# Weight pieces of 512 rows by 512 columns in place of 1024 rows by 256 columns, in a one-core streaming encoder step

## What is computed

```python
def trunk_layer(x, k_cache, v_cache, s0, pos0, ...):
    h = rms_norm(x, attn_norm_g)
    proj = h @ w_in                                   # 1024 x 2816
    ...
    x = x + mixed @ w_out                             # 1024 x 1024
    x = x + peer(rms_norm(x, ffn_norm_g), peer_w_q, peer_sub_keys, peer_u, peer_v)

def peer(x, w_q, sub_keys, u_table, v_table):         # for each block of 128 tokens
    q = (xblk @ w_q).reshape(PEER_BLOCK, PEER_HEADS, 2, PEER_HALF)      # 1024 x 2048
    ...                                               # top 16 of 128 keys twice, then top 16 of 256: 128 experts a token
    u = u_table[expert]
    hid = jax.nn.gelu(jnp.einsum('thkd,td->thk', u, xblk).astype(jnp.float32), approximate=False)
    v = v_table[expert]
    return jnp.einsum('thk,thkd->td', (g * hid).astype(xblk.dtype), v)
```

## Time and profile before

| | us |
|---|---|
| median of 3 runs | 3637.41 (3636.71 to 3653.42) |
| the profiled execution, its own time | 3651.41 |
| its span, first to last instruction | 3649.3 |
| busy: PE / PE weight loads / DVE / ACT / POOL | 1989.2 / 1092.7 / 2038.2 / 324.0 / 2103.3 |
| mean rate of the DMA engines over the span | 352 GB/s |
| bytes of the POOL queue (q0) / of SP's queue (q1) | 1140.99 MB / 134.48 MB |

### The profile page before, as it was taken

How to read it: one execution, slowest core, us unless ns; L and a number is a source line. 1 busy time by engine, 2 the same in 40 slices (tenths; PEclk the granted TensorE clock), 3 DMA queues, 4 the chain that set the end, 5 groups by cost and what they waited for, 6 DMA issues and landing times. The chain is left out here.

```text
span 3649.3 us, 27702 instructions
## 1 busy us (share of the span) xinstructions
PE 1989.2 (55%) x9448; PEld 1092.7 (30%) x9448; DVE 2038.2 (56%) x4571; ACT 324.0 (9%) x778; POOL 2103.3 (58%) x2183
## 2 busy tenths in 40 slices
PE   6975563766673447657734367557634332223446
PEld 6764441544550115324501034324301000000001
DVE  2379747567648674674565744755675644444120
ACT  2211010111100010111100010101000000000000
POOL 0045523656556675665566765666676766666665
PEclk9986786886885668768956579668756655655669
DMA  6588965999999999999999999999998999999998
GB/s 224 179 302 287 392 234 184 343 397 355 381 383 376 371 368 395 401 368 367 397 394 353 344 378 394 392 370 394 404 349 328 368 376 375 373 364 386 366 362 323
DMA packets 442170, 1286.15 MB, mean 352 GB/s; under 512 B 39408, under 2 KB 157936, under 8 KB 442032
## 3 DMA queue, kind: packets, MB, share of 16 engines
q0 software_dynamic: 313344, 1140.99, 82.0%
q1 hardware_dynamic: 126224, 134.48, 11.0%
q10 hardware_dynamic: 2464, 8.91, 0.6%
HBM read 1274.50 MB, written 9.44 MB: 352 GB/s over the span
## 5 line engine op out<-in xcount | busy, mean ns | idle before, releaser
L926 DVE CUSTOM_DVE_ANT_0 ring<-ring,ps 128x1024 f32<-128x1024 f32 x1088 | 1298.2, 1218 | 929.7 <-DMA ring<-in_peer_u_dram,u_idx 777.6
L658 POOL DMA_INDIRECT ring<-in_peer_u_dram,u_idx x1088 | 1038.6, 955 | 809.4 <-issue 286.4
L1243 PE MATMUL ps<-ring,spread 128*32 128x512 f32 x4352 | 884.2, 916 | 1122.5 <-DMA ring<-in_peer_v_dram,v_idx 1011.2
L658 POOL DMA_INDIRECT ring<-in_peer_v_dram,v_idx x1088 | 1062.9, 977 | 718.6 <-issue 292.9
L1284 PE MATMUL ps<-wbuf,actT 128*128 128x256 f32 (+1 forms) x2944 | 712.0, 401 | 135.4 <-issue 94.9
L1243 PEld LDWEIGHTS ps<-ring,spread 128*32 128x32 f32 x4352 | 180.5, 143 | 1717.8 <-issue 1700.9
L1284 PEld LDWEIGHTS ps<-wbuf,actT 128*128 128x128 f32 (+1 forms) x2944 | 563.0, 195 | 317.5 <-issue 213.6
L999 DVE MAX8 work<-work 128x8 f32<-128x128 f32 (+3 forms) x432 | 109.6, 325 | 84.5 <-ACT work L895 68.0
L1003 DVE FIND_INDEX8 work<-work 128x8 uint32<-128x128 f32 (+3 forms) x432 | 134.3, 335 | 15.6 <-issue 15.6
L728 ACT COPY spread<-weightT 128x16 f32<-128x16 f32 x64 | 14.0, 219 | 924.6 <-PE ps L1243 487.6
L926 DVE DVE_READ_ACCUMULATOR2_ANT hidden<- 128x1 f32 x1088 | 90.2, 83 | 1.1 <-issue 1.1
(11 more groups left out here) (153 smaller groups left out, 1283.8 us busy)
## 6 DMA issues: line engine op xcount, KB each, us to landing
wbuf<-in_w_in_dram SPq DMA_DIRECT2D x55, 1024.0 KB
wbuf<-in_peer_w_q_dram SPq DMA_DIRECT2D x40, 1024.0 KB
wbuf<-in_w_out_dram SPq DMA_DIRECT2D x20, 1024.0 KB
ring<-in_peer_u_dram,u_idx POOLq DMA_INDIRECT x1088
ring<-in_peer_v_dram,v_idx POOLq DMA_INDIRECT x1088
x_v<-x_scratch ACTq DMA_DIRECT2D x8, 512.0 KB
out_dram<-x_v ACTq DMA_DIRECT2D x8, 512.0 KB
x_in<-in_x_prompt_dram SPq DMA_DIRECT2D x7, 512.0 KB
```

Of the source, the lines that this page charges most:

```text
L658: pool.indirect_dma_start(ring[:, at % RING, :], None, table, bass.IndirectOffsetOnAxis(ap=idx, axis=0)).then_inc(landed[at % RING], 16)
L926: ch.put(v_.tensor_tensor_reduce(out=row, in0=row, in1=ux_ps, scale=1.0, scalar=0.0, op0=ALU.mult, op1=ALU.add, accum_out=hidden[:, k:k + ...
L1243: mm = pe.matmul(ps[j:j + 32, B_ACC + c, :], spread[:, at:at + 32], tile[:, 512 * c:512 * c + 512], start=(t % 32 == 0), stop=(t % 32 == 3 ...
```

## The change

A piece is now half the rows (512) by twice the columns (512), still 1 MB, but 512 runs of 2 KB. A product of 512 columns is made of two half sums: for both blocks the first half of k from one piece, then for both blocks the second half from the next. `w_in` has 2816 columns, so its last 256 columns stay one piece of 1024 rows. There are 23 pieces in a phase as before (11 of `w_in`, 4, 8), 6 + 2 + 4 products of a block in place of 11 + 4 + 8, and half as many matmuls of twice the width. A product fills a whole PSUM bank. The first half's end is signalled by a new semaphore `half_used`, on which SP refills. The copies and adds are 512 columns wide; they come at the point of `Pace` at which the second half of the block is done. `EARLY` is 4 of the 512-column products, `PIECE` is 7.2.

```diff
-WCOLS = 256
-N_IN, N_OUT, N_Q = IN_W // WCOLS, D // WCOLS, 2 * PH * 128 // WCOLS
-PIECES = N_IN + N_OUT + N_Q
+WCOLS = 512
+N_IN, N_OUT, N_Q = -(-IN_W // WCOLS), D // WCOLS, 2 * PH * 128 // WCOLS
 WRING = 3
-EARLY = 8
-EARLY_LOADS = EARLY + 2
+EARLY = 4
...
+def pieces():
+    out = []
+    for name, count, width in (("w_in", N_IN, IN_W), ("w_out", N_OUT, D), ("w_q", N_Q, 2 * PH * 128)):
+        for p in range(count):
+            whole = width - p * WCOLS < WCOLS
+            out += [(name, p, half) for half in ((None,) if whole else (0, 1))]
+    return out
...
-    NORM, PIECE, ATTN, PEER, BEGUN_PEER = 6, 3.6, 55, 105, 58
+    NORM, PIECE, ATTN, PEER, BEGUN_PEER = 6, 7.2, 55, 105, 58
...
-        wbuf = sb("wbuf", [P, WRING, KC, WCOLS])
+        wbuf = sb("wbuf", [P, WRING, KC // 2 * WCOLS])
...
+                elif n >= WRING:
+                    name, p, half = W_PIECES[n - WRING]
+                    if half == 0:
+                        firsts = sum(h == 0 for _, _, h in W_PIECES[:n - WRING + 1])
+                        grp = next(i for i, phase in enumerate(PHASES) if phase[0] == blocks)
+                        sp.wait_ge(half_used, grp * (N_IN - 1 + N_OUT + N_Q) + firsts)
+                    elif name == "w_in":
+                        sp.wait_ge(in_done, N_IN * b0 + (p + 1) * G)
...
-                        th.step("w_in", m, 0.5)
+                        th.step("w_in", p * G, (G + g + 1) / 2)
...
-                        th.step("w_q", m, 0.5)
+                        th.step("w_q", p * G, (G + g + 1) / 2)
...
-                        th.step("w_out", m, 0.5)
+                        th.step("w_out", p * G, (G + g + 1) / 2)
...
+            def products(grp, name, p, blocks, free, signal):
+
+                G = len(blocks)
+                parts = halves(name, p)
+                for i, (n, half) in enumerate(parts):
+                    last = i == len(parts) - 1
                     for g, b in enumerate(blocks):
+                        m, T = p * G + g, rows(b)
+                        th.step(name, p * G, (i * G + g) / len(parts))
+                        if i == 0:
+                            free(g, b, m)
+                        pe.wait_ge(w_landed[n % WRING],
+                                   16 * (grp * len(range(n % WRING, PIECES, WRING)) + n // WRING + 1))
+                        w = w_place(n)
+                        ks = range(KC) if half is None else range(half * (KC // 2), (half + 1) * (KC // 2))
+                        for k in ks:
+                            if k == ks[len(ks) // 2]:
+                                th.step(name, p * G, (i * G + g + 0.5) / len(parts))
+                            mm = pe.matmul(ps[0:T, 2 + m % 2, 0:w.shape[-1]], act_of[b][:, k, 0:T], w[:, k - ks[0], :],
+                                           start=(k == 0), stop=(k == KC - 1), skip_group_check=True)
+                        if last:
+                            mm.then_inc(signal, 1)
+                        elif g == G - 1:
+                            mm.then_inc(half_used, 1)
```

More of the change, by code:

```diff
@@ L66, with halves @@
 RING = 14
+def pieces():
[5 more added lines that the diff above has]
+    return out
+W_PIECES = pieces()
+PIECES = len(W_PIECES)
+IN_PIECES = sum(name == "w_in" for name, _, _ in W_PIECES)
+OUT_PIECES = sum(name == "w_out" for name, _, _ in W_PIECES)
+EARLY_LOADS = 2 * EARLY + 2
+def halves(name, p):
+    return [(n, half) for n, (m, c, half) in enumerate(W_PIECES) if (m, c) == (name, p)]
 SLOPES = [2.0 ** (-8.0 * (h + 1) / HEADS) for h in range(HEADS)]
@@ L292, in hymba_peer_program @@
     u_table, v_table = peer_u[0], peer_v[0]
-    w_views = [w[0].rearrange("(k p) n -> p k n", p=P) for w in (w_in, w_out, peer_w_q)]
+    w_views = {name: w[0].rearrange("(k p) n -> p k n", p=P)
+               for name, w in (("w_in", w_in), ("w_out", w_out), ("w_q", peer_w_q))}
     def w_piece(n):
[L296 to L302, removed]
+        name, p, half = W_PIECES[n]
+        if half is None:
+            return w_views[name][:, :, p * WCOLS:]
+        return w_views[name][:, half * (KC // 2):(half + 1) * (KC // 2), p * WCOLS:(p + 1) * WCOLS]
     def x_rows(b):
@@ L512, in hymba_peer_program @@
         following = PHASES[1][0]
[L513 removed]
+        early_h = {1: 0, 2: 1}
         order = gather_order()
@@ L547, in stream @@
                     m = n - WRING
[L548 to L553, removed]
+                    if m == IN_PIECES:
                         for g, b in enumerate(blocks):
                             if b >= SAMPLE - 1:
-                                th.step("attn", g, 1.0)
                                 store_window_and_state(b)
-                    if m == N_IN + N_OUT:
+                    if m == IN_PIECES + OUT_PIECES:
                         for g, b in enumerate(blocks):
-                            th.step("norm2", g)
                             T = rows(b)
@@ L1263, in h_transposed, with project @@
                     transposed(i, T, lambda c: h_nat[0:T, (4 * i + c) * P:(4 * i + c + 1) * P], 4, h_tr)
-            def project(blocks, grp, pieces):
+            def project(blocks, grp, chunks):
                 G = len(blocks)
-                for p in pieces:
-                    for g, b in enumerate(blocks):
-                        m = p * G + g
-                        th.step("w_in", m)
-                        pe.wait_ge(hT_ready, 2 * b + 2)
-                        if m >= 2:
-                            pe.wait_ge(proj_ready, N_IN * blocks[0] + m - 1)
-                        product(grp, "w_in", 0, p, m, b, in_done)
@@ L1277, in product, with free @@
-            def product(grp, name, first, p, m, b, signal):
-                n, T = first + p, rows(b)
-                pe.wait_ge(w_landed[n % WRING], 16 * (grp * len(range(n % WRING, PIECES, WRING)) + n // WRING + 1))
-                for k in range(KC):
-                    if k == KC // 2:
-                        th.step(name, m, 0.5)
-                    mm = pe.matmul(ps[0:T, 2 + m % 2, 0:WCOLS], act_of[b][:, k, 0:T], wbuf[:, n % WRING, k, :],
-                                   start=(k == 0), stop=(k == KC - 1))
-                mm.then_inc(signal, 1)
+                def free(g, b, m):
+                    pe.wait_ge(hT_ready, 2 * b + 2)
+                    if m >= 2:
+                        pe.wait_ge(proj_ready, N_IN * blocks[0] + m - 1)
```

80 lines of the change are left out of this document (41 added, 39 removed).

## The result

| | before | after |
|---|---|---|
| median of 4 runs, us | 3638.5 (3636.7 to 3653.4) | 3593.5 (3583.1 to 3604.0) |
| the profiled execution / its span, us | 3651.4 / 3649.3 | 3583.1 / 3581.2 |

What follows compares the result with a forecast made beforehand. Bound by the chain of products, attention and top-16 search until about 650 us, then by the DMA engines. Terms: -15 - 4 - 3 + 1 = -21 us, from 3637 to 3616 us; forecast's own range 3600 to 3634, overall 3594 to 3648.

Steps and rivals of the forecast that it cites:

- `w_q`, -3 us: Phase 1's `w_q`, where PE waits for ACT's copies: one product more done by 453 us, -3 us (+7 to -10).
- `w_out`, -4 us: Phase 1's one 4.34 us wait for a `w_out` piece: pieces land in 7.3 us, not 12.1, -4 us (0 to -4).
- Packets, -15 us: Weights from 660 us on: fewer packets, each with a fixed cost of 7.3 ns, -15 us (0 to -31).
- mixed rate: Sign of being right: where weights and gathers fill the DMA queues, the sum rises from 394 to 400 GB/s or more.
- Width of the matmuls, 0 us: PE: four matmuls of 512 columns take the same 3.45 us as eight of 256, no change; upper end +4 us.
- Copies +1, joints, order 0: Wider last copies at step ends in phases 0 and 1 cost +1 us; shifted order of items costs nothing.
- Run length not what limits: Rival: full DMA engines give about 400 GB/s whatever the packets; only phase 1 and copies count, 3631 us, chance 0.22.
- Fewer joints help: Rival: half as many copies joining products save waiting on something unnamed throughout, 25 us more, 3591 us, chance 0.12.
- Stiffer joints: Rival: PE wants the bank sooner after its copy and loses half products in phases 2 to 4, 3659 us, chance 0.16.
- pace of wide matmuls: Sign of being right: on PE, four wide matmuls take 3.45 us.
- phase 1 ends 5 to 10 us earlier: Sign of being right: the end of phase 1 comes 5 to 10 us earlier.
- all of ACT's waits for an unnamed releaser grew: Sign of being wrong: ACT's waits for which the profile names no releaser grow; no size given.

Runs made afterwards that it cites:

- e3: The change's joints, copies and order with 1 KB packets and 256-column matmuls of the kernel before, noisy chip: ratio 1.002 to the kernel before.
- e2: The change with each wide matmul as two of 256 columns, alternating column halves, each with its own start, noisy chip: ratio 1.0004 to the kernel before.
- e1_runs_2k: The change with each piece moved by two DMAs of row halves, still 2 KB packets, noisy chip: ratio 0.9892 to the kernel before.
- e1_runs_1k: The change with each piece moved by two DMAs of column halves, so 1 KB packets, noisy chip: ratio 0.9944 to the kernel before.
- e13: e1_runs_2k again, as control on a quiet chip: 3364.5 us, ratio 0.9862 to the kernel before.
- e11: e13 with 1 KB packets for the weights of phase 1 alone: 3391.0 us, ratio 0.9941 to the kernel before.
- e12: e13 with 1 KB packets for the weights of phases 2 to 4 alone: 3383.7 us, ratio 0.9923 to the kernel before.
- c2: The kernel before, unaltered, run for its profile on a quiet chip: ratio 0.9996.
- e8: The change with each half product as two 256-column halves one behind the other, sums started once a bank, quiet chip: ratio 0.9861 to the kernel before.
- e6: The change with four empty PE instructions ahead of each wide matmul, quiet chip: ratio 0.9859 to the kernel before.
- e9: e3 unaltered on a quiet chip: ratio 0.9994 to the kernel before.
- e7: The change with a matmul of 4 zero columns behind each wide one, quiet chip: ratio 1.0039 to the kernel before.
- e4: The change with each half product as two 256-column halves one behind the other, each with its own start, quiet chip: ratio 0.9861 to the kernel before.

## Why the prediction was wrong

**`w_q`, -3 us: the step that failed.** The prediction let ACT's late copies hold PE until 453 us as before and gave the change one product more by then. In its own pair of executions `w_q` became 28 us shorter, and its unnamed stops fell from 31.9 to 7.1 us. What took them away stays open. It was not that pieces came sooner. The earlier trace rows show it: from 430 to 450 us the weights' queue moved nothing, so the pieces that had been issued had landed, while PE stood the 16.70 us that ended at 453.13. Ahead of the stop of 15.19 us that began at 416.16, the queue moved 10 packets from 405 to 410 us, so the third piece, issued at 390.50 and wanted next, lay ready as well. By the traces of the noisy chips, one execution of each kernel, it goes with the width of the matmuls: the last unnamed stop ends at 453.1, 453.6 and 456.0 us with narrow ones (before, e3, e2), and at 424.5, 443.6 and 443.4 with wide ones (the change, e1_runs_2k, e1_runs_1k).

On the quiet chips, where no such stop exists, the same term fails for a reason that is shown. The pieces are the limit there. From e13 to e11 only the packets of phase 1 differ, and `w_q` is 57.0 and 77.8 us long. The first three pieces lie ready in the ring; the fourth comes 3.1 us late, the next three follow every 12.4 us in place of 7.1, which makes 19 of the 20.8 us; for the last the gathers have run out. The prediction had this arithmetic, 12.1 us a piece with 1 KB and 7.3 with 2 KB, and applied it only to the wait that the trace named, in `w_out`. The Trainium skill ("DMA: Bandwidth & Descriptors", "Queues, rings and completion order") has the rule in general: an engine goes round the queues that have work, a whole packet from each. The trace agrees, 2961 packets to 2962. The page calls 9 to 17 descriptors in a packet typical; equal counts would come out with any number that both queues share, so the trace neither shows nor refutes that.

**`w_out`, -4 us: right.** e11 has a wait of 2.88 us there and begins `w_q` 3.7 us after e13.

**Packets, -15 us: right in kind, somewhat small.** e12 measures 19.2 us for phases 2 to 4. The 7.3 ns for a packet were 9: by the line through three sizes above, and by e12, 19.2 us x 16 over 33,792 packets saved = 9.1 ns. That a 2 KB packet costs the same as one of 1 KB, the term's condition, is shown by that line. The mixed rate rose as foretold, from 394 to 402 GB/s in c2's and the change's stretches. The skill's rule that was weighed against it (the Trainium skill, "DMA: Bandwidth & Descriptors", "Why small descriptors are slow"; an estimate of 9 us) came out too low.

**Width of the matmuls, 0 us: right on the quiet chips, not on the noisy one.** Four wide ones take 6.87 / 2 = 3.43 us in phase 0 against 3.45 forecast, and e8 equals the change. (The upper end counted 20 wide half products in phase 0; there are 22, which makes no difference to the sum.) On the chip of e1 to e3, e2 loses everything that the packets give: the term put at nothing is there as large as the whole gain. Two limits would fit, late completions of products with narrow matmuls and, once they are gone, late pieces; this is argued, not shown. Why completions are late on some chips, and less so with half the matmuls, no run here shows; e6 was meant to and could not. e2 also alternates column halves and gives their starts in its own way, and neither was taken out on a noisy chip.

**Copies +1, joints, order 0: right.** e9 gives -0.1%, within its interval, and e3 +0.2%. DVE's add behind "weights" and the stiffer joints cost no more than that.

**The rivals.** "Run length not what limits" is refuted by the table of four. "Fewer joints help" had the right time, 3591, by luck, and the wrong cause: the joints alone give nothing. "Stiffer joints" did not happen. Of the signs listed, the packets, the mixed rate, the pace of wide matmuls and the tail came as said; "phase 1 ends 5 to 10 us earlier" did not, it was 40, and that line pointed at the failed step. One sign of being wrong came too: all of ACT's waits for an unnamed releaser grew, from 735.5 to 866.4 us, though those of the product copies fell from 253.8 to 61.5. They end in other places, the copy into `spread` above all (332.2 to 589.0 us), and the run was faster all the same, so this sum was no measure of the time.

## What to carry to other kernels

When two DMA queues are both full, count what each gets in packets, not in bytes: here the share of the weights' queue was its packet size over the sum of both sizes, and doubling its run from 1 to 2 KB nearly halved the time to land a piece (22.4 to 11.8 us), with 2% more bandwidth in all. Then apply that to every piece whose step is on the path, not only to the one wait that the profile names. Where a stop has an unnamed releaser, first look whether the queue that could explain it was moving anything during the stop, then ask what would end it next if it were gone; a second chip may show that bare.

## What the runs showed of the hardware

- The same program took 3409 to 3411 us on two chips and 3640 to 3660 on others. In the faster ones' profiles no wait ends on "remote", and the tail runs at 409 GB/s (3000 to 3300 us, c2) where the earlier trace rows have 372.
- A packet of weights cost 9 ns beside its bytes at 512 bytes, 1 KB and 2 KB alike: 291, 348 and 387 GB/s where weights moved alone.
- The two queues alternated packet for packet at 512 bytes, 1 KB and 2 KB alike: 2668 to 2669, 2961 to 2962, 2141 to 2141.
- A matmul of 4 columns with its own load of 128x128 float32 weights took 222 ns of PE's path in phase 0 (e7).
- A start for one column range of a PSUM bank, given while the sum of another range of the same bank was open, made that other range drop what it had summed; with the first range closed before (e9) it did not. The Trainium skill ("PSUM — Partial Sum Buffer", "The four PSUM rules") says so, and the trace has no say in it; the time is not touched, since e4 and e8 take the same.
